# Second attention of a two-block kernel: separate order plans for VectorE and ScalarE, values of two query blocks together, and the gating constant from sums of rows

## The chip, the cores and the metric

The kernel runs on one core of a Trainium2 chip. The metric is the device time of one execution in microseconds (us), the median of several runs. The engines of the core are TensorE (PE: matmuls; PEld: its weight loads), VectorE (DVE), ScalarE (ACT), GpSimd (POOL) and SyncE (SP, which here only issues DMAs). Each engine works through its own list of instructions in order; they meet only through semaphores.

## The reference, cut to what matters

Two transformer blocks run one after the other over 512 positions of width 1024, all in float32. The change touches two places of the second block:

```python
def gmlp_spatial_gating(z_u, z_v, ln_g, ln_b, w_s, b_s):
    v = layernorm(z_v, ln_g, ln_b)               # ... * g + b, per channel c
    w = where(mask, w_s, 0)                      # 8 groups, 128 x 128
    mixed = einsum('gts,bnsgc->bntgc', w, v) + b_s.T[None, None, :, :, None]
    return z_u * mixed

def forgetting_attention(q, k, v, f_logit, b_f): # 16 heads of 64, query blocks of 128
    for i in range(4):
        s = q[block i] . k[: end of block i] / 8 + cum[t] - cum[s]
        s = where(causal, s, -1e30)
        prob = softmax(s)
        out[block i] = prob . v
```

The bias `ln_b` of the layernorm goes through `w_s` as a constant that doesn't depend on the data: for group g, channel c and position t it is ln_b[g, c] * sum over s of w[g, t, s], plus b_s[g, t]. The kernel works this "gating constant" `e_s` out early, stores it in DRAM and loads it back when the gating is due.

## The kernel before, in words

Activations lie transposed, channels on the 128 partitions, 512 positions in the free dimension. Every weight tile (128 x 1024) is loaded by SP into one of a few raw buffers, and split: ScalarE writes a rounded high part (`split_hi`, L1111), VectorE the rest (`prepare`, L1572). A product is three matmuls (high times high, low times high, high times low), each at one pass with 512 columns, so a tile of eight chunks takes 24 matmuls, all issued at L609. There are six split buffers, so a split may run up to six tiles ahead of its use; a raw buffer is loaded again once its tile is split.

**The second attention** is woven into 20 main tiles (480 matmuls at L609). Its unit of work is n = 0 .. 63: four query blocks of two heads for each of eight pairs c = n // 8; i = n % 8 // 2 is the query block, so a unit has 128 (i+1) key columns. For each unit:

1. TensorE, `fox_scores(n)`: two score matmuls (L781, L784) and a small bf16 mask matmul (L989) into bank 4 or 5.
2. VectorE, `fox_scores(n)` (L2020): adds the decay row, writes `at_p`, takes the row minimum.
3. ScalarE, `fox_scores(n)` (L1452): exponential, with the row sum.
4. VectorE: reciprocal (L2023) and scaling of `at_p` (L2025).
5. TensorE, `fox_turn(n)` (L1000): i+1 transposes of full precision into the one bank 6. It waits for step 4 of the unit and for step 6 of unit n-1.
6. ScalarE, `fox_turn(n)` (L1459): copy out to `at_pt`.
7. TensorE, `fox_values(n)` for odd n (L1014): for both heads of the pair, products of full precision with `at_pt`, each on half of the array's columns (128*64).

`mix2_order` (L255) writes one list of events for all engines. Step n of it issues turn n-2, scores n and, where n is odd, values n-4, in this order, and then lets through some main matmuls (`woven`, L213): 5 to 9 for each step. Where a main tile ends, the list has "evac" (ScalarE and VectorE take it out of its bank: for a tile of queries two half-tiles each, L1226 and L1753; for keys two half-tiles each, L1235 and L1761, and two copies on VectorE, L1765) and "end" (one weight tile is split, L1111 and L1572). All three engines walk the same list, so on VectorE the pieces of "evac" and "end" stand as one block between two units, and steps 2 and 4 of a unit stand together: between them VectorE waits for step 3.

Queries and keys of pair c are double-buffered; TensorE may start scores of pair c when all their pieces are done.

**The gating constant** is made by `constant(x)` on TensorE (L842), called within the first feed-forward behind unit m = 7 of 22. For each of the eight groups it is a product `lnb` x `ws_s` (L851, contraction over 128 rows) and a product of a row of ones with the row `bs_row` (L852, contraction over one row), both of full precision. ScalarE copies the two banks to `e_s` (L1321), GpSimd stores it.

## Time and profile before

| | us |
|---|---|
| median of 3 runs | 2108.72 (2106.93 to 2109.04) |
| the profiled execution: its own time | 2107.84 |
| its span in the trace | 2106.0 |
| TensorE busy in the span | 2054.4 |
| VectorE busy | 1104.9 |
| ScalarE busy | 807.7 |
| mean granted clock of TensorE | 0.991 of full speed |

The span is the time from the first to the last record of the trace; the execution's own time has 1.84 us around it. The second attention lies between 1260.7 and about 1450 us of the span, the gating constant between 133.96 and 140.98 us.

In a timeline a row is a run of equal instructions: start, length from the first start to the last end, engine, line, what is written from what, shape, count, and in brackets the idle time before it with the engine and line that ended it. Full-precision products show two records for each matmul. Ends of matmuls are modelled; starts are not.

### The profile page before, as it was taken

What the parts mean: (1) busy time and instruction counts of PE and PEld (TensorE: products, weight loads), DVE (VectorE), ACT (ScalarE), POOL (GpSimd) and SP (SyncE); (2) the same over time, 40 slices, a digit from 0 to 9 for tenths busy, and PEclk for the clock granted to TensorE, in tenths of its full rate; (3) what the DMA queues carried; (4) which work ended last, traced back from release to release, by engine and by line L of the source; (5) the groups of instructions that cost most, each with busy time, mean ns of one, the idle gap of its engine ahead of it and who ended that gap; (6) DMA issues with size and microseconds to landing.
All of it is one profiled execution on the core that took longest, in us unless ns stands there. A gap on an engine that the chain in (4) does not pass through costs nothing.

```text
span 2106.0 us, 25140 instructions
## 1 busy us (share of the span) xinstructions
PE 2054.4 (98%) x10227; PEld 1714.1 (81%) x10227; DVE 1104.9 (52%) x1678; ACT 807.7 (38%) x1256; POOL 116.0 (6%) x139
## 2 busy tenths in 40 slices
PE   6999999999999999999999999999999999999997
PEld 4788888888888888888888887778888888888887
DVE  8734444577854554333335546664524476446546
ACT  4422222345544333222224345555323354234334
POOL 3100000100000010000002000000000100000012
PEclk8999999999999999999999999999999999999999
DMA  7744443433432323233223332222332222232241
GB/s 279 248 146 148 172 149 125 166 122 117 142 110 92 98 61 120 75 103 112 88 70 100 112 114 81 71 71 83 98 99 91 81 95 87 90 119 94 69 148 41
DMA packets 70164, 236.27 MB, mean 112 GB/s; under 512 B 7825, under 2 KB 10129, under 8 KB 69666
## 3 DMA queue, kind: packets, MB, share of 16 engines
q1 hardware_dynamic: 67874, 226.59, 32.3%
q0 software_dynamic: 2032, 7.90, 1.1%
q8 instruction: 81, 1.33, 0.3%
q10 hardware_dynamic: 144, 0.18, 0.0%
q14 instruction: 33, 0.27, 0.0%
HBM read 229.89 MB, written 4.75 MB: 111 GB/s over the span
## 4 chain that ended last, share of the span: by engine, by line
PE 90%; DVE 5%; ACT 2%; DMA 1%; issue 1%; POOL 0%; DVEq 0%; SPq 0%; ACTq 0%
PE bank L609 80%; PE bank L673 4%; PE bank L896 1%; DVE w_lo L1572 1%; PE bank L1014 1%; PE bank L1000 1%; ACT at_p L1452 1%; PE bank L781 1%; PE bank L784 1%; DVE raw_m L1568 1%; DMA w_raw<-in_w_mix_dram 0%; PE bank L926 0%; DVE at_p L2020 0%; DVE ssq L1588 0%; DVE klb L1761 0%
## 5 line engine op out<-in xcount | busy, mean ns | idle before, releaser
L1572 DVE TENSOR_TENSOR w_lo<-w_raw,w_hi 128x1024 fp32r<-128x1024 f32 (+2 forms) x367 | 418.4, 1168 | 215.7 <-ACT w_hi L1111 214.8
L609 PE MATMUL bank<-u_lo,w_hi 128*128 128x512 f32 (+1 forms) x1920 | 496.9, 371 | 11.7 <-DVE u_lo L1852 4.9
L609 PE MATMUL bank<-u_hi,w_hi 128*128 128x512 f32 (+1 forms) x1920 | 499.3, 373 | 8.7 <-ACT ff_s L1191 3.6
L609 PE MATMUL bank<-u_hi,w_lo 128*128 128x512 f32 (+1 forms) x1920 | 496.5, 371 | 0.0
L1111 ACT ACTIVATE w_hi<-w_raw 128x1024 fp32r<-128x1024 f32 (+2 forms) x368 | 347.4, 976 | 260.2 <-PE bank L609 194.8
L609 PEld LDWEIGHTS bank<-u_lo,w_hi 128*128 128x128 f32 x1920 | 357.1, 189 | 75.7 <-DVE u_lo L1852 5.7
L609 PEld LDWEIGHTS bank<-u_hi,w_hi 128*128 128x128 f32 x1920 | 358.5, 190 | 72.2 <-ACT ff_s L1191 4.0
L609 PEld LDWEIGHTS bank<-u_hi,w_lo 128*128 128x128 f32 x1920 | 358.6, 190 | 60.9 <-issue 1.7
L1690 DVE TENSOR_TENSOR ff_a<-ff_s,bank 128x512 f32<-128x512 f32 x44 | 30.3, 688 | 233.1 <-issue 220.2
L1185 ACT ACTIVATE act_hi<-ff_a 128x512 fp32r<-128x512 f32 x66 | 41.7, 632 | 256.8 <-DVE ff_a L1690 216.7
L609 PE MATMUL bank<-act_hi,w_lo 128*128 128x512 f32 (+1 forms) x561 | 131.4, 379 | 0.0
L609 PE MATMUL bank<-act_lo,w_hi 128*128 128x512 f32 (+1 forms) x561 | 130.0, 378 | 0.0
L609 PE MATMUL bank<-act_hi,w_hi 128*128 128x512 f32 (+1 forms) x561 | 129.4, 376 | 0.0
L2150 POOL TENSOR_TENSOR ssq<-ssq,sq 128x512 f32<-128x512 f32 (+1 forms) x41 | 50.6, 1235 | 1371.9 <-ACT sq L1136 1371.2
L609 PEld LDWEIGHTS bank<-act_hi,w_lo 128*128 128x128 f32 x561 | 102.1, 189 | 19.3
L609 PEld LDWEIGHTS bank<-act_lo,w_hi 128*128 128x128 f32 x561 | 102.0, 190 | 19.3
L609 PEld LDWEIGHTS bank<-act_hi,w_hi 128*128 128x128 f32 x561 | 101.4, 188 | 19.5
L1568 DVE CUSTOM_DVE_ANT_0 w_raw<-w_raw,cact_t,vecs_t 128x1024 f32<-128x1024 f32 x66 | 87.2, 1327 | 0.4 <-DMA w_raw<-in_w_ada_dram 0.4
L1136 ACT ACTIVATE sq<-hres 128x512 f32<-128x512 f32 (+1 forms) x60 | 33.0, 552 | 116.3 <-DVE hres L1660 68.9
L1716 DVE TENSOR_TENSOR act_lo<-ff_a,act_hi 128x512 fp32r<-128x512 f32 x66 | 45.8, 693 | 51.1 <-ACT act_hi L1185 51.1
L1705 DVE SCALAR_TENSOR_TENSOR ff_c<-bank,vecs_t,ff_c 128x511 f32<-128x511 f32 (+1 forms) x44 | 33.0, 749 | 60.3 <-ACT ff_c L1199 59.4
L1191 ACT ACTIVATE ff_s<-bank 128x512 f32<-128x512 f32 x44 | 26.2, 595 | 94.2 <-PE bank L609 94.2
(273 smaller groups left out, 2129.4 us busy)
## 6 DMA issues: line engine op xcount, KB each, us to landing
w_raw<-in_w_gu_dram SPq DMA_DIRECT2D x127, 512.0 KB, 4.0
w_raw<-in_w_ada_dram SPq DMA_DIRECT2D x66, 512.0 KB, 4.5
w_raw<-in_w_dn_dram SPq DMA_DIRECT2D x48, 384.0 KB, 3.1
w_raw<-in_w_mix_dram SPq DMA_DIRECT2D x36, 512.0 KB, 3.9
w_raw<-in_w_dn_dram SPq DMA_DIRECT2D x48, 320.0 KB, 3.2
w_raw<-in_w_in_dram SPq DMA_DIRECT2D x24, 512.0 KB, 3.5
w_raw<-in_w_o_dram SPq DMA_DIRECT2D x16, 512.0 KB, 3.5
w_raw<-in_w_in_g_dram SPq DMA_DIRECT2D x16, 512.0 KB, 3.5
```

Of the source, the lines that this page charges most:

```text
L609: m = e.matmul(bank[b][:, c], w, (x.lo if part == 2 else x.hi)[:, k, c], start=start, stop=stop, skip_group_check=True)
L673: m = e.matmul(bank[b][:, :], (x.lo if part == 1 else x.hi)[:, k, P * i:P * (i + 1)], w, start=k == 0 and part == 0, stop=k == 2 * len(til ...
L1111: e.activation(hi_of(name), raw_of(i), ACT.Copy).then_inc(*s_w_hi.inc(name))
L1136: e.activation((sq, sq2)[x][d % 2][:, c], hres[:, d, c], ACT.Square, **kw).then_inc(*s_sq.inc(*keys))
L1185: e.activation(act_hi[:, i, :], ff_a[m % 3][:, :], ACT.Copy).then_inc(*s_a_hi.inc((tag, h, i)))
L1191: e.activation(ff_s[m % 3][:, :], psum(f"{tag}g{m}")[:, :], ACT.Silu).then_inc(*s_silu.inc((tag, m)))
L1568: e.tensor_tensor_reduce(raw_of(i), raw_of(i), cact[:, :], 1.0, vecs[:, c:c + 1], ALU.mult, ALU.add, mod[:, name:name + 1]).then_inc(*s_ad ...
L1572: e.tensor_tensor(lo_of(name), raw_of(i), f32(hi_of(name)), ALU.subtract).then_inc(*s_w_lo.inc(name))
L1690: e.tensor_tensor(ff_a[m % 3][:, :], ff_s[m % 3][:, :], psum(f"{tag}u{m}")[:, :], ALU.mult).then_inc(*s_glu.inc((tag, m)))
L1705: e.scalar_tensor_tensor(dst[:, n:T], src[:, 0:T - n], vec("conv_w_2", 44 * k + col), dst[:, n:T], ALU.mult, ALU.add).then_inc(*s_conv.inc ...
L1716: e.tensor_tensor(act_lo[:, i, :], ff_a[m % 3][:, :], f32(act_hi[:, i, :]), ALU.subtract).then_inc(*s_a_lo.inc((tag, h, i)))
L2150: e.tensor_tensor(ssq[x][:, c], ssq[x][:, c], (sq, sq2)[x][d % 2][:, c], ALU.add).then_inc(*s_ssq_pool.inc(*keys))
```

## The change: what it does

- `mix2_order`: the values of two query blocks stand together, in step n with n % 4 = 2, ahead of the turn: values n-5 and n-3 there, then turn n-2, scores n. The order ends after 67 steps rather than 68.
- `mix2_scalar_order` and `mix2_vector_order` (new) derive an own list for ScalarE and VectorE. What "evac" and "end" asked for is cut into pieces (half a tile of queries or keys, one copy, one split, one result) in a queue. ScalarE does one piece behind each scores, two where more than two are left. VectorE does one piece between step 2 and step 4 of a unit (`divide`, cut off from `fox_scores`), and a second one behind step 4 where more than two are left; it takes a piece only if ScalarE has its part in an earlier step.
- The gating constant: two full-precision matmuls of 512 columns with a stationary tile of ones sum the masked rows of `ws_s`; VectorE (no longer ScalarE) forms sum * lnb + bs in eight instructions behind unit m = 8. `bs_all` is now the row b_s broadcast to 128 partitions (512 KB, as `lnb` was before), `lnb` a [128, 8] tile loaded one word at a time (1024 words).

The signatures and declarations around it (`ps=BOTH`, `lnb_t`, the removed `one_row`) are left out of the diff:

```diff
@@ -257,14 +258,14 @@
     steps = []
-    for n in range(64 + 4):
+    for n in range(64 + 3):
         s = []
+        if n >= 6 and n % 4 == 2:
+            s += [("values", n - 5), ("values", n - 3)]
         if 2 <= n < 66:
...
             s.append(("scores", n))
-        if n >= 5 and n % 2:
-            s.append(("values", n - 4))
         steps += [s] + [[]] * (share[n % 8] - 1)
@@ -286,6 +287,65 @@
     return out
+def mix2_scalar_order(events):
+    out, later, when = [], deque(), {}
+    def piece(n):
+        if later:
+            when[later[0]] = n
+            out.append(later.popleft())
+    for what, i in events:
+        j = MIX2[i] if what in ("evac", "end") else 0
+        if what == "evac":
+            later.extend([("zu", i)] if j < 8 else [("query" if j < 24 else "key", (j, p)) for p in BOTH])
+        elif what == "end":
+            later.append(("split", i))
+        elif what == "turn":
+            out.append(("turn", i))
+        elif what == "scores":
+            out.append(("scores", i))
+            piece(i)
+            if len(later) > 2:
+                piece(i)
+    while later:
+        piece(64)
+    return out, when
+def mix2_vector_order(events, when):
+    out, later = [], deque()
+    def piece(n):
+        if later and later[0][1] < n:
+            out.append(later.popleft()[0])
+    for what, i in events:
+        j = MIX2[i] if what in ("evac", "end") else 0
+        if what == "evac" and 8 <= j < 24:
+            later.extend((("query", (j, p)), when["query", (j, 1)]) for p in BOTH)
+        elif what == "evac" and j >= 24:
+            later.extend((("key", (j, p)), when["key", (j, 1)]) for p in BOTH)
+            later.extend((("copy", (j, p)), when["key", (j, 1)]) for p in BOTH)
+        elif what == "end":
+            later.append((("split", i), when["split", i]))
+        elif what == "values" and i % 8 == 7:
+            later.appendleft((("result", i), 0))
+        elif what == "scores":
+            out.append(("scores", i))
+            piece(i)
+            out.append(("divide", i))
+            if len(later) > 2:
+                piece(i)
+    while later:
+        piece(65)
+    return out
 def gating_order():
@@ -842,16 +903,10 @@
             open_bank(b)
+            q.wait_ge(s_const, "eps")
             q.wait_ge(s_ws_mask, 0)
-            q.wait_ge(s_lnb_in, 0)
-            q.wait_ge(s_bs_in, 0)
-            for i in range(4):
-                g = 4 * x + i
-                o = bank[b][:, P * i:P * (i + 1)]
-                e.matmul(o, lnb[:, P * g:P * (g + 1)], ws_s[:, g, :], start=i == 0, stop=False, skip_group_check=True)
-                m = e.matmul(o, one_row[:, :], bs_row[:, P * g:P * (g + 1)], start=False, stop=True,
-                             skip_group_check=True)
-            m.then_inc(*s_out.inc(("const", x)))
+            e.matmul(bank[b][:, :], ones[:, :].to_broadcast([P, P]), ws_s[:, 4 * x:4 * x + 4, :].rearrange("p g c -> p (g c)"),
+                     start=True, stop=True, skip_group_check=True).then_inc(*s_out.inc(("const", x)))
             frees[b] = [(s_e, x)]
@@ -1216,21 +1269,21 @@
                         pump(name)
-        def queries(ph, c, key, scale):
+        def queries(ph, c, key, scale, ps=BOTH):
             s = c % 2
...
                 q.wait_ge(s_out, ("scores", 2 * c - 3, A0) if ph == "a" else ("fox", 8 * c - 9))
-            for p in range(2):
+            for p in ps:
                 own = slice(64 * p, 64 * p + 64)
                 e.activation(qs_t[s][p][own, :], psum(key)[own, :], ACT.Copy, scale=scale).then_inc(*s_q_hi.inc((ph, c, p)))
-        def keys(ph, c, key):
+        def keys(ph, c, key, ps=BOTH):
             s = c % 2
...
                 q.wait_ge(s_out, ("scores", 2 * c - 3, A0) if ph == "a" else ("fox", 8 * c - 9))
-            for p in range(2):
+            for p in ps:
                 own = slice(64 * p, 64 * p + 64)
@@ -1314,13 +1367,7 @@
                 split_hi()
-
-        def constants():
-            for x in range(2):
-                q.wait_ge(s_out, ("const", x))
-                e.activation(e_s[:, 4 * x:4 * x + 4, :], rows_view[6 + x], ACT.Copy).then_inc(*s_e.inc(x))
-
-        ffn("1", "n1", swiglu, beside=constants)
+        ffn("1", "n1", swiglu)
         q.wait_ge(s_e_out, 0)
@@ -1460,17 +1507,18 @@
         table(LOG_EXP)
-        for what, i in mix2_events:
-            if what == "evac":
+        for what, i in mix2_scalar:
+            if what == "zu":
                 j = MIX2[i]
-                if j < 8:
-                    q.wait_ge(s_out, (f"n{j}", None))
-                    e.activation(zu[j][:, :], psum(f"n{j}")[:, :], ACT.Copy).then_inc(*s_zu.inc(j))
-                elif j < 24:
-                    queries("b", j % 8, f"n{j}", -0.125)
-                else:
-                    keys("b", j % 8, f"n{j}")
-            elif what == "end":
+                q.wait_ge(s_out, (f"n{j}", None))
+                e.activation(zu[j][:, :], psum(f"n{j}")[:, :], ACT.Copy).then_inc(*s_zu.inc(j))
+            elif what == "query":
+                j, p = i
+                queries("b", j % 8, f"n{j}", -0.125, (p,))
+            elif what == "key":
+                j, p = i
+                keys("b", j % 8, f"n{j}", (p,))
+            elif what == "split":
                 pump(f"n{MIX2[i]}")
@@ -1722,8 +1770,8 @@
                     pump(f"{tag}u{max(m, first_pairs[tag] - 1)}")
-                    if beside and m == 5:
-                        beside()
+                    if beside and m in beside:
+                        beside[m]()
                 if h == 0 and half:
@@ -1745,22 +1793,29 @@
                         pump(key + "b")
-        def queries(ph, c, key, scale):
+        def queries(ph, c, key, scale, ps=BOTH):
             s = c % 2
             q.wait_ge(s_q_hi, (ph, c, 1))
-            for p in range(2):
+            for p in ps:
                 own, other = slice(64 * p, 64 * p + 64), slice(64 - 64 * p, 128 - 64 * p)
...
         def keys(ph, c, key):
+            key_lows(ph, c, key)
+            key_copies(ph, c)
+        def key_lows(ph, c, key, ps=BOTH):
             s = c % 2
             q.wait_ge(s_k_hi, (ph, c, 1))
-            for p in range(2):
+            for p in ps:
                 own = slice(64 * p, 64 * p + 64)
                 e.tensor_tensor(kl_t[ph][s][p][own, :], psum(key)[own, :], f32(ks_t[s][p][own, :]),
                                 ALU.subtract).then_inc(*s_kl.inc((ph, c, p)))
-            for p in range(2):
+        def key_copies(ph, c, ps=BOTH):
+            s = c % 2
+            for p in ps:
                 own, other = slice(64 * p, 64 * p + 64), slice(64 - 64 * p, 128 - 64 * p)
@@ -1859,7 +1913,20 @@
             e.memset(ws_s[64:128, :, 0:64], 0.0).then_inc(*s_ws_mask.inc(0))
-        ffn("1", "n1", swiglu, lambda d, h: x_ready("n0", d), half_gate(0), half=(0, 0), beside=constant_mask)
+        def constants():
+            q.wait_ge(s_lnb_in, 0)
+            q.wait_ge(s_bs_in, 0)
+            for x in range(2):
+                q.wait_ge(s_out, ("const", x))
+                for i in range(4):
+                    g = 4 * x + i
+                    m = e.scalar_tensor_tensor(e_s[:, g, :], bank[6 + x][:, P * i:P * (i + 1)], lnb[:, g:g + 1],
+                                               bs_all[:, g, :], ALU.mult, ALU.add)
+                m.then_inc(*s_e.inc(x))
+        ffn("1", "n1", swiglu, lambda d, h: x_ready("n0", d), half_gate(0), half=(0, 0),
+            beside={5: constant_mask, 8: constants})
         q.wait_ge(s_e_out, 0)
@@ -2019,23 +2086,32 @@
                                    mneg[:, col]).then_inc(*s_fmin.inc(n))
+        def fox_divide(n):
+            i, p = n % 8 // 2, n % 2
+            pt, col = at_p[p][:, 0:P * (i + 1)], slice(n % 8, n % 8 + 1)
             q.wait_ge(s_fexp, n)
...
             e.tensor_scalar(pt, pt, rinv[:, col], None, op0=ALU.mult).then_inc(*s_fe.inc(n))
-        for what, i in mix2_events:
-            if what == "evac":
-                j = MIX2[i]
-                if 8 <= j < 24:
-                    queries("b", j % 8, f"n{j}", -0.125)
-                elif j >= 24:
-                    keys("b", j % 8, f"n{j}")
-            elif what == "end":
+        for what, i in mix2_vector:
+            if what == "query":
+                j, p = i
+                queries("b", j % 8, f"n{j}", -0.125, (p,))
+            elif what == "key":
+                j, p = i
+                key_lows("b", j % 8, f"n{j}", (p,))
+            elif what == "copy":
+                j, p = i
+                key_copies("b", j % 8, (p,))
+            elif what == "split":
                 pump(f"n{MIX2[i]}")
             elif what == "scores":
                 fox_scores(i)
-            elif what == "values" and i % 8 == 7:
+            elif what == "divide":
+                fox_divide(i)
+            elif what == "result":
                 q.wait_ge(s_out, ("values", "b", i))
@@ -2309,8 +2385,9 @@
         e.dma_start(ws_s[:, :, :], io["ws"]).then_inc(*s_ws_in.inc(0, by=16))
-        e.dma_start(lnb[:, :], io["ln_b"].to_broadcast([P, D])).then_inc(*s_lnb_in.inc(0, by=16))
-        e.dma_start(bs_row[:, :], io["b_s"]).then_inc(*s_bs_in.inc(0, by=16))
+        e.dma_start(bs_all[:, :, :].rearrange("p g c -> p (g c)"), io["b_s"].to_broadcast([P, D])).then_inc(*s_bs_in.inc(0, by=16))
+        with nc.allow_non_contiguous_dma("one word of the norm's bias for each partition and group"):
+            e.dma_start(lnb[:, :], io["ln_b"].rearrange("o (g c) -> c (o g)", c=P)).then_inc(*s_lnb_in.inc(0, by=16))
         e.dma_start(b_f[:, :], io["b_f"]).then_inc(*s_bf_in.inc(0, by=16))
```

## Rows read from the trace of the kernel before

**Rows 1.** The page, busy us of each engine (share of the span).

```profile
PE 2054.4 (98%) x10227; PEld 1714.1 (81%) x10227; DVE 1104.9 (52%) x1678; ACT 807.7 (38%) x1256; POOL 116.0 (6%) x139
```

**Rows 2.** Windows, whole second attention: from:to, length, busy us per engine, PEclk.

```profile
1260.70:1449.00 188.30, 181.43 (x1126) 140.22 (x1125) 114.28 (x320) 104.40 (x244) 6.56 (x12) 1.00 0.23 71
```

**Rows 3.** Waits, same stretch: who waits for whom, us, times, longest.

```profile
DVE rinv_t L2023 <- ACT at_p L1452: 46.2, 64, 0.9
...
PE bank L1000 <- DVE at_p L2025: 6.1, 6, 1.3
...
PE bank L1000 <- ACT at_pte L1459: 0.6, 1, 0.6
```

**Rows 4.** Timeline of TensorE: start us, us, line, tiles, count, idle before.

```profile
1290.38 1.84 PE L609 MATMUL bank<-u_hi,w_lo 128*128 128x512 f32 x7
1293.56 0.41 PE L1000 MATMUL bank<-ident_t,at_p 128*128 128x128 f32 x2 [1.33 <-DVE at_p L2025]
```

**Rows 5.** Timeline of VectorE ahead of that idle.

```profile
1288.16 1.41 DVE L1761 TENSOR_TENSOR klb<-bank,ks 64x512 fp32r<-64x512 f32 x2 [0.55 <-ACT ks L1235]
1289.60 0.88 DVE L1765 CAST ks<-ks 64x512 fp32r<-64x512 f32 x2
1290.51 1.23 DVE L1572 TENSOR_TENSOR w_lo<-w_raw,w_hi 128x1024 fp32r<-128x1024 f32 x1
1291.76 0.42 DVE L2020 CUSTOM_DVE_ANT_0 at_p<-bank,at_c 128x256 f32<-128x256 f32 x1
```

**Rows 6.** Timeline of TensorE: mask to second main matmul, three steps.

```profile
1276.52 0.23 PE L989 MATMUL bank<-mask_b,ident_b 128*128 128x128 bf16 x1
...
1277.60 2.00 PE L609 MATMUL bank<-u_hi,w_hi 128*128 128x512 f32 x8
...
1297.22 0.23 PE L989 MATMUL bank<-mask_b,ident_b 128*128 128x128 bf16 x1
...
1297.57 2.02 PE L609 MATMUL bank<-u_hi,w_hi 128*128 128x512 f32 x8
...
1359.45 0.23 PE L989 MATMUL bank<-mask_b,ident_b 128*128 128x128 bf16 x1
...
1360.98 1.11 PE L609 MATMUL bank<-u_hi,w_lo 128*128 128x512 f32 x4
```

**Rows 7.** Timeline of TensorE: values straight behind main matmuls.

```profile
1449.19 0.63 PE L609 MATMUL bank<-u_lo,w_hi 128*128 128x512 f32 x2
1449.75 1.09 PE L1014 MATMUL bank<-at_pto,v_b 128*64 128x128 f32 x16
```

**Rows 8.** Timeline of VectorE: one step of 512 columns.

```profile
1276.79 0.69 DVE L2020 CUSTOM_DVE_ANT_0 at_p<-bank,at_c 128x512 f32<-128x512 f32 x1 [0.30 <-PE bank L989]
...
1278.57 0.49 DVE L2025 TENSOR_SCALAR at_p<-at_p,rinv_t 128x512 f32<-128x512 f32 x1
```

**Rows 9.** Timeline of TensorE around the gating constant.

```profile
133.96 0.38 PE L851 MATMUL bank<-ws_s,lnb 128*128 128x128 f32 x2
...
140.98 3.78 PE L609 MATMUL bank<-u_hi,w_hi 128*128 128x512 f32 x8
...
147.39 1.99 PE L609 MATMUL bank<-u_lo,w_hi 128*128 128x512 f32 x8
...
149.21 1.07 PE L609 MATMUL bank<-u_hi,w_hi 128*128 128x512 f32 x4
```

**Rows 10.** Windows, last us of the constant.

```profile
140.00:141.00 1.00, 1.00 (x5) 0.55 (x4) 0.11 (x2) 0.00 (x0) 0.00 (x0) 0.50 0.73 121
```

**Rows 11.** Timeline of TensorE: four full-precision products of 128 columns.

```profile
1457.71 1.05 PE L1046 MATMUL bank<-ws,zv 128*128 128x128 f32 x8
...
1458.52 2.07 PE L609 MATMUL bank<-u_hi,w_hi 128*128 128x512 f32 x8
```

**Rows 12.** Timeline of VectorE in the first feed-forward.

```profile
134.22 0.69 DVE L1690 TENSOR_TENSOR ff_a<-ff_s,bank 128x512 f32<-128x512 f32 x1 [4.98 <-issue]
```

**Rows 13.** The page, DMA queues: packets, MB, share of 16 engines.

```profile
q1 hardware_dynamic: 67874, 226.59, 32.3%
```

13 lines of the change are left out of this document (6 added, 7 removed).

## The prediction

> **What bounds the kernel now.** I read the busy times first. TensorE is busy 2054.4 of 2106.0 us, VectorE and ScalarE about half and a third [rows 1]. So a change pays only where it shortens what TensorE issues, where TensorE stands idle, or where its clock is low; work taken from VectorE or ScalarE is worth what TensorE stops waiting for.
>
> Then the windows. In the second attention TensorE is busy 181.43 of 188.30 us at full clock [rows 2]: 6.87 us idle. The waits name it: transposes (L1000) wait six times for VectorE's scaling of at_p (6.1 us, at most 1.3 each), once for ScalarE's copy (0.6) [rows 3], and once more for 0.2. There are eight such gaps. A gap is longer than its bracket, because ends are modelled. Main matmuls start 0.2275 us apart (eight in 1.82 us, the last two of [rows 9]). In the gap shown [rows 4] the second of seven starts 0.35 us behind its mask (below), so the eighth start would be at about 1292.05; the transpose starts at 1293.56: 1.5 us, not 1.33. With 0.2 us more for each of eight gaps the stalls are 8.3 us.
>
> What makes them is in VectorE's list ahead of the gap [rows 5]: 1.41 us of keys, 0.88 of copies and 1.23 of a split stand in one block, 3.6 us from 1288.16 to 1291.76, and only then comes step 2 of the next unit. Meanwhile VectorE itself waited 46.2 us in the stage, 64 times up to 0.9, for ScalarE's exponential between its steps 2 and 4 [rows 3].
>
> Last, the timeline and the clock around the gating constant. TensorE has left the main matmuls at 133.96 and is back at 140.98 [rows 9]: 7.02 us for 16 small products. In the last of these us the granted clock is 0.50, so 1.2 GHz instead of 2.4 [rows 10], and the two groups of eight behind it take 147.39 - 140.98 = 6.41 us where sixteen at full clock take 3.64 [rows 9]: 2.77 us more. TensorE was not idle before the clock fell; it had issued 6 us of short products, every second over one row of the array.
>
> **The change, part by part.**
>
> *1. Gating constant, TensorE.* Removed: 7.02 us. Added: two full-precision matmuls of 512 columns. Four full-precision products of 128 columns on the whole array, 512 columns together, take 1458.52 - 1457.71 = 0.81 us [rows 11], so two of 512 are 1.62. With about 0.2 us for entering and leaving I take 1.8. The bounds are half of it and double: 0.9, if those rows are held up by their eight weight loads and not by the columns, and 3.5, if the clock is at 1.2 GHz. Saved: 5.2 (3.5 to 6.1).
>
> *2. Gating constant, clock.* With full-height, full-width matmuls in place of the short ones I expect no fall at 140 us: 2.77 us saved. The bounds are 0 (it falls all the same) and 3.3 (0.5 us of the constant also ran slow, already in part 1). I take 2.8. Parts 1 and 2 together: 8.0.
>
> *3. Gating constant, elsewhere.* ScalarE loses two copies, which no one waited for. VectorE gains eight instructions of 128 columns; the nearest row is 0.42 us for 256 columns [rows 5], so at most 3.4 us. They stand behind unit m = 8, where VectorE then waits 5 us for TensorE in each unit [rows 12]; that wait hides them. If the cover were gone they would cost up to 3.4. GpSimd stores the constant a few us later, and it is wanted only at the end of the first feed-forward and again 1300 us later. On SP's queue the broadcast keeps its size, but the 1024 words of lnb are new: every weight load behind them waits. A packet of this queue takes 0.323 * 16 * 2106 / 67874 = 0.16 us on average [rows 13]; 64 on each of 16 engines would be at most 10 us. Five split tiles of 24 * 0.2275 = 5.46 us stand ahead of TensorE, 27 us, so 10 us are hidden. I take 0, and keep the other end for a rival.
>
> The Trainium skill ("DMA: Bandwidth & Descriptors", section "Why a DMA increments its semaphore by 16 and not by 1") lets the slowest dimension of both sides, here 128, set how many engines share a transfer: 16. By that rule the delay is the hidden one; a transfer of so small pieces is not in the trace of before, so no row here shows it yet.
>
> *4. Values in pairs.* A values group between a mask and main matmuls costs TensorE more than its matmuls. From mask to second main matmul it is 0.35 us without values (1297.22 to 1297.57), 1.08 with eight records (1276.52 to 1277.60), 1.53 with sixteen (1359.45 to 1360.98) [rows 6]. So eight cost 0.73 and sixteen 1.18: 0.056 for each record and 0.28 fixed for the group. Half as many groups (16 for 32) save 16 * 0.28 = 4.5 us, if a pair costs one fixed part. Now the group stands behind main matmuls of 512 columns, not behind a small mask, and ahead of a transpose. The entry is the same: behind two main matmuls the values start at 1449.75, where the third would have started at 1449.65 [rows 7]. The exit into a transpose is in no row; it may cost its weight load more, some 0.1 us, 1.6 over sixteen. I take 4.0 (bounds 1.0 and 4.5).
>
> The Trainium skill ("TensorEngine Tiling (Array Packing)", section "Tiling Modes", "Key Properties") says that a change of tiling mode drains the engine. By it a group entered behind 512 columns would drain longer than behind 128 and the pair would save little; the entry of 0.1 us in rows 7 speaks against that, and by the rule's strictest reading the sum would be 3 us smaller.
>
> *5. Own orders for VectorE and ScalarE.* Walking the new list step by step: VectorE never has more than two pieces in a unit, and one of them lies in a gap of up to 0.9 us in which it used to wait. A heavy unit (512 columns) was 1.79 us from step 2 to the start of step 4, plus 0.49 [rows 8], so 2.3; with a split in the gap it is 2.6, with one more half-tile 3.3, against 2.3 + 3.6 before. TensorE gives a unit 2.9 us there (nine main matmuls 2.05, transposes, scores) and two units of slack before the transposes need step 4. Light units (256 columns) last 1.7 us on TensorE and 1.9 to 2.6 on VectorE, but only two in a row, and then comes a pair of values (0.28 + 28 * 0.056 = 1.8 us). So the eight gaps go.
>
> What is late next: (a) scores 32. In the new list the last copy of keys of pair 4 stands behind step 4 of unit 31, and scores 32 wait for it. VectorE is through at 0.27 + 2.27 + 0.44 = 3.0 us behind mask 31, TensorE arrives after nine main matmuls and four transposes, 2.5 us: 0.5 us idle. In all other pairs the last copy stands earlier. (b) ScalarE does turn n-1 behind exp n and a piece, and turn n waits for that copy; where VectorE is two us behind, around units 12 to 16, I expect some 1.5 us in all. Stalls left: 2.0 us (bounds 0.5 and 8). Saved: 8.3 - 2.0 = 6.3.
>
> No cost: the weight splits are done up to two steps later, with five tiles ahead (27 us); banks of main tiles are free at least four steps before they are opened again; behind the last values the order is as before.
>
> **Sum.** 8.0 + 4.0 + 6.3 = 18.3. The profiled execution took 2107.84 (span 2106.0 and 1.84 around it), so 2089.5; its own time is 0.9 below the median shown, so I give the median of the changed kernel as 2090, with 2085 to 2094 for this case alone.
>
> **The rivals.**
>
> *A. The clock still falls at the constant, or falls in the attention.* For it: it fell without idle time before. Against it: at full clock all through the attention, with eight stalls of up to 1.5 us [rows 2]. Price 2.8: 2093.
>
> *B. New waits take the place of the old ones.* Pieces between steps 2 and 4 hold up step 4: a split is 1.23 us [rows 5] in a gap of at most 0.88, so 0.35 later each time; over 20 splits 7.0 us, if every one reaches TensorE. That eats part 5: 2096.5. For it: the transposes already wait for just this result. Against it: two units of slack.
>
> *C. Slower: the 1024 words go through one DMA engine.* Then the loads behind them are held by 1024 * 0.16 = 164 us less 27 of cover: 137 us of standing TensorE, 2227. It decides from where the words hold the queue over 27 + 18 = 45 us, so if fewer than four engines share them or a word costs four times a mean packet. For it: no transfer like it in the trace. Against it: broadcasts over 128 partitions landed as any other load, and the new one is over 128 partitions too.
>
> *D. The values don't pair on TensorE (each pays its fixed part).* 4.0 less: 2094.
>
> **How the numbers follow.** Chances: my forecast 0.62, A 0.09, B 0.15, C 0.03, D 0.09, other small losses 0.02. The range of 8 in 10 leaves out C and part of B: 2084 to 2097. Faster by over 0.2% (4.2 us, about what a measurement of this kernel can tell from no change) needs only a quarter of the sum: 0.95; the same 0.015, slower 0.035.
>
> **What would show it right or wrong.** TensorE between its last main matmul before the constant and the first after it: 1.8 us; clock 1.00 in the 10 us after. Attention: idle of TensorE 1 to 2 us instead of 6.87, one of the gaps ahead of L781 of scores 32, waiting for L1765; 16 blocks of L1014 with 0.26 to 0.36 fixed each; VectorE's wait before L2023 down from 46 to about 20 us. The prediction is wrong if the stage shortens by less than 6 us, if the clock shows 0.50 behind the constant, or if weight splits (L1111) wait for DMA between 110 and 130 us.

## The result and the profile after

The changed kernel takes 2085.06 us (median of four, 2082.51 to 2085.57), the kernel before 2108.41 in the same comparison: ratio 0.9888, 95% interval 0.9871 to 0.9905. That is 23.4 us off, where 18.3 were forecast, and by the interval 20.0 to 27.2; 2085.06 lies in the range of 2084 to 2097, near its lower end. The profiled execution took 2082.51, with a span of 2080.4 us.

The page after, busy us of each engine and the large DMA queue, beside [rows 1] and [rows 13]: TensorE does 14 us less work in a span 25.6 us shorter, and the queue carries 1038 packets more in about the same share of time (32.6 and 32.3%).

```profile
PE 2040.0 (98%) x10199; PEld 1705.3 (82%) x10199; DVE 1106.4 (53%) x1685; ACT 806.8 (39%) x1254; POOL 116.3 (6%) x139
...
q1 hardware_dynamic: 68912, 226.59, 32.6%
```

TensorE around the constant, beside [rows 9], and the window of [rows 10] again. The two matmuls (four records) take 133.56 - 132.25 = 1.31 us; the eight main matmuls behind them take 2.25 for the usual 1.82, 0.43 more. Together 1.74. The clock stays at 1.00.

```profile
132.25 1.88 PE L908 MATMUL bank<-ws_s,ones_t 128*128 128x512 f32 x4
133.56 2.41 PE L670 MATMUL bank<-u_hi,w_hi 128*128 128x512 f32 x8
135.81 1.99 PE L670 MATMUL bank<-u_hi,w_lo 128*128 128x512 f32 x8
```

```profile
140.00:141.00 1.00, 1.00 (x6) 0.84 (x5) 0.00 (x0) 0.24 (x1) 0.00 (x0) 1.00 1.00 406
```

VectorE's eight instructions for `e_s` cost 0.27 us each (the timeline of VectorE, behind unit m = 8):

```profile
150.08 2.16 DVE L1924 SCALAR_TENSOR_TENSOR e_s<-bank,lnb_t,bs_all 128x128 f32<-128x128 f32 x8
```

The window of the second attention without its first and last pieces, beside [rows 2]: TensorE is idle 0.37 us, 6.87 before.

```profile
1248.80:1424.30 175.50, 175.13 (x1116) 137.58 (x1115) 112.62 (x319) 103.01 (x243) 6.58 (x12) 1.00 0.25 76
```

The waits there, beside [rows 3]. L2094 is the line that was L2023, L842 was L781. VectorE's wait for the exponential went from 46.2 us in 64 pieces to 18.7 in 34, since pieces now fill it; in return it waits 35.4 us for the next scores: it is early. TensorE has one wait left.

```profile
DVE at_p L2087 <- PE bank L1044: 35.4, 34, 2.3
DVE rinv_t L2094 <- ACT at_p L1499: 18.7, 34, 0.9
...
PE bank L842 <- DVE ks L1820: 0.3, 1, 0.3
```

That wait on TensorE's timeline, and VectorE's beside it. Scores 32 wait for the second copy of keys, which stands behind `divide` of unit 31 (the TENSOR_SCALAR). Unhindered, they would start 0.35 to 0.36 us behind the first of the four transposes, at 1333.13 (as at 1270.36 and 1270.71 in the fence after this one); they start at 1333.71, 0.58 late.

```profile
1332.77 0.60 PE L1055 MATMUL bank<-ident_t,at_p 128*128 128x128 f32 x4
1333.71 0.30 PE L842 MATMUL bank<-ks,qs 128*128 128x128 f32 x1 [0.35 <-DVE ks L1820]
```

```profile
1332.62 0.49 DVE L2096 TENSOR_SCALAR at_p<-at_p,rinv_t 128x512 f32<-128x512 f32 x1
1333.14 0.42 DVE L1820 CAST ks<-ks 64x512 fp32r<-64x512 f32 x1
```

A pair of values on TensorE's timeline, behind five main matmuls: twelve and sixteen records in one block, entered and left once.

```profile
1270.36 0.60 PE L1055 MATMUL bank<-ident_t,at_p 128*128 128x128 f32 x4
1270.71 0.31 PE L842 MATMUL bank<-ks,qs 128*128 128x128 f32 x1
...
1271.01 1.40 PE L670 MATMUL bank<-u_lo,w_hi 128*128 128x512 f32 x5
1272.34 0.88 PE L1069 MATMUL bank<-at_pte,v_b 128*64 128x128 f32 x12
1273.05 1.04 PE L1069 MATMUL bank<-at_pto,v_b 128*64 128x128 f32 x16
1274.02 0.33 PE L1055 MATMUL bank<-ident_t,at_p 128*128 128x128 f32 x1
```

**Where the time went, stage by stage.** The chain of waits joins unbroken work of TensorE into blocks (start us, us, engine, tile, line, records). Four of them recur in every trace and serve as marks. Of before:

```profile
141.05 271.37 PE bank L609 x1200
...
630.01 140.68 PE bank L609 x655
...
1173.43 87.04 PE bank L673 x384
...
1479.39 196.01 PE bank L609 x900
```

and of after:

```profile
134.12 268.53 PE bank L670 x1200
...
616.62 140.68 PE bank L670 x655
...
1161.57 87.04 PE bank L734 x384
...
1454.70 196.01 PE bank L670 x900
```

From the first product of the constant (133.96, 132.25) to the end of the first block: 278.46 and 270.40 us, 8.06 less. From the end of the 87.04 block to the start of the 196.01 block, which is the second attention: 218.92 and 206.09, 12.83 less. These two hold what the change touches. The other 4.7 us of the two spans lie outside it: 3.6 of them between the first block and the 140.68 one (217.59 and 213.97), 1.7 ahead of the constant (133.96 and 132.25), 0.9 behind the start of the 196.01 block, and 1.5 the other way between the starts of the 140.68 block and the 87.04 one (543.42 and 544.95). The experiments had to tell what of all this is the change's.

### The profile page after: what moved, and what is told of

Same layout as the page of the kernel before. It is cut to its first block, busy times and chain, and to the rows that moved or that the text cites. A ratio compares the mean times of both kernels' runs of the same rounds, so it can differ in the third digit from the quotient of the medians.

```text
span 2080.4 us, 25071 instructions
## 1 busy us (share of the span) xinstructions
PE 2040.0 (98%) x10199; PEld 1705.3 (82%) x10199; DVE 1106.4 (53%) x1685; ACT 806.8 (39%) x1254; POOL 116.3 (6%) x139
## 3 DMA queue, kind: packets, MB, share of 16 engines
q1 hardware_dynamic: 68912, 226.59, 32.6%
q8 instruction: 81, 1.33, 0.3%
## 4 chain that ended last, share of the span: by engine, by line
PE 94%; DVE 3%; ACT 1%; DMA 1%; issue 0%; POOL 0%; DVEq 0%; SPq 0%; ACTq 0%
PE bank L670 82%; PE bank L734 5%; PE bank L1069 1%; PE bank L1055 1%; PE bank L951 1%; PE bank L842 1%; PE bank L845 1%; DVE raw_m L1616 1%; DMA w_raw<-in_w_gu_dram 0%; PE bank L981 0%; DVE w_raw L1616 0%; DVE ssq L1636 0%; PE bank L1101 0%; PE bank L755 0%; PE bank L764 0%
## 5 line engine op out<-in xcount | busy, mean ns | idle before, releaser
L734 PE MATMUL bank<-w_hi,u_hi 128*128 128x512 f32 x160 | 62.3, 389 | 0.0
```

The source lines that it names most:

```text
L734: m = e.matmul(bank[b][:, :], (x.lo if part == 1 else x.hi)[:, k, P * i:P * (i + 1)], w, start=k == 0 and part == 0, stop=k == 2 * len(til ...
```

## The experiments

Medians are of runs beside the kernel before on one chip, and a ratio is to its median there: 2108.41 beside the changed kernel, 2107.60 beside constant alone to tall constant, 2108.15 beside gap unused to attention alone, 2106.84 beside the last three. "Constant" and "attention" are the two stretches just defined, and "between" the one from the end of the first block to the start of the 140.68 one, from each kernel's own trace.

| kernel | median us | ratio to before [95%] | constant | between | attention |
|---|---|---|---|---|---|
| before | 2108.41 | | 278.46 | 217.59 | 218.92 |
| changed | 2085.06 | 0.9888 [0.9871, 0.9905] | 270.40 | 213.97 | 206.09 |
| constant alone | 2096.39 | 0.9952 [0.9940, 0.9965] | 270.41 | 213.38 | 218.96 |
| pairs alone | 2106.64 | 0.9996 [0.9986, 1.0006] | 279.85 | 214.72 | 218.74 |
| plans alone | 2099.67 | 0.9964 [0.9951, 0.9977] | 279.90 | 218.10 | 210.46 |
| tall constant | 2100.15 | 0.9967 [0.9955, 0.9978] | 272.23 | 216.13 | 218.92 |
| gap unused | 2092.39 | 0.9926 [0.9913, 0.9940] | 270.40 | 213.32 | 213.89 |
| copy early | 2085.09 | 0.9894 [0.9878, 0.9910] | 270.41 | 214.32 | 205.52 |
| changed again | 2084.65 | 0.9890 [0.9876, 0.9904] | 270.41 | 214.15 | 206.09 |
| attention alone | 2095.54 | 0.9941 [0.9928, 0.9953] | 279.89 | 215.24 | 206.11 |
| before again | 2111.62 (one) | | 279.91 | 218.33 | 218.95 |
| more words | 2107.64 | 1.0001 [0.9989, 1.0013] | 279.86 | 213.98 | 218.93 |
| constants moved | 2084.91 | 0.9901 [0.9885, 0.9917] | 270.41 | 215.23 | 206.10 |
| few words | 2083.75 | 0.9890 [0.9875, 0.9906] | 270.41 | 214.18 | 206.08 |

**Constant alone.** The new constant and its loads in the kernel before:

```diff
-                e.matmul(o, lnb[:, P * g:P * (g + 1)], ws_s[:, g, :], start=i == 0, stop=False, skip_group_check=True)
-                m = e.matmul(o, one_row[:, :], bs_row[:, P * g:P * (g + 1)], start=False, stop=True,
...
+            e.matmul(bank[b][:, :], ones[:, :].to_broadcast([P, P]), ws_s[:, 4 * x:4 * x + 4, :].rearrange("p g c -> p (g c)"),
...
```

> The kernel before with the new gating constant alone; the attention keeps its old order. Theory 1 (the parts add): TensorE is away from its main matmuls for about 1.7 us instead of 7.02, the clock shows 1.00 behind it, the eight gaps of the attention (6.9 us of idle) stay; 8.0 us faster, so 2100 to 2101. Rival (the clock's fall is only moved, because it comes where it comes in any order): 5.3 us faster, and a stretch at 0.50 shows within the 10 us behind the constant. Rival of the 1024 words: weight splits wait for DMA between 105 and 130 us.

Measured: 270.41 in the constant's stretch, the attention unchanged. TensorE's timeline has the same rows as the changed kernel, 1.31 us and then the 2.41 us group:

```profile
134.15 1.88 PE L846 MATMUL bank<-ws_s,ones_t 128*128 128x512 f32 x4
135.46 2.41 PE L608 MATMUL bank<-u_hi,w_hi 128*128 128x512 f32 x8
```

Theory 1 held. The ratio says 10.1 us (7.4 to 12.6 by its interval, so 8.06 is not excluded); before again (below) shows why it may be more than 8.06.

**Tall constant.** The old constant, with its second product over 128 rows (`lnb` and `ws_s` again) in place of one row, so that `b_s` is left out of it:

```diff
-                m = e.matmul(o, one_row[:, :], bs_row[:, P * g:P * (g + 1)], start=False, stop=True,
+                m = e.matmul(o, lnb[:, P * g:P * (g + 1)], ws_s[:, g, :], start=False, stop=True,
```

> The kernel before, where the second product of each group of the constant (a row of ones with the row of b_s, contraction over one row) is the first product once more, over 128 rows; b_s is left out of the result. Sixteen small full-precision products as before, all on the whole array. Theory A (the one-row products make it slow and let the clock fall): 16 products at about 0.2 us, 3.3 us instead of 7.02, no clock of 0.50 behind it: 3.7 + 2.8 = 6.5 us faster. Theory B (short products in themselves do both): still about 7 us, clock 0.50 behind it, no difference in time. Between them: 3.3 us, but the clock falls all the same: 3.7 faster.

The same count of products of the same width, but each pair of records starts 0.22 us behind the last (0.31 once and then 0.41 to 0.42 with the one-row products in between, up to the clock's fall, as in before again below), the whole is 136.46 - 132.97 = 3.49 us, and the clock is 1.00 throughout. The timeline of TensorE, first two products, last, and what follows:

```profile
132.97 0.38 PE L851 MATMUL bank<-ws_s,lnb 128*128 128x128 f32 x2
133.19 0.39 PE L852 MATMUL bank<-ws_s,lnb 128*128 128x128 f32 x2
...
136.31 0.39 PE L852 MATMUL bank<-ws_s,lnb 128*128 128x128 f32 x2
136.46 2.07 PE L609 MATMUL bank<-u_hi,w_hi 128*128 128x512 f32 x8
```

So without the one-row products both losses are gone, the slow issue and the clock fall; the stretch is 7.7 us shorter than in the other traces of the old constant (279.9, below), where Theory A said 6.5. The two wide matmuls save another 1.8 us (272.23 - 270.41). Two things stay open. The steps of 0.41 us go from a one-row product to a full one as well as the other way, so the rows don't tell whether the one-row product itself is slow or the change between the two shapes. And the products are through in 3.49 us here, while in the six traces of the old constant the clock fell 3.1 to 5.9 us behind the first of them: that the shorter stretch, and not its full height, kept the clock up is not excluded by this one trace.

**Pairs alone.** Only `mix2_order` as in the change, the engines' orders as before:

```diff
+        if n >= 6 and n % 4 == 2:
+            s += [("values", n - 5), ("values", n - 3)]
-        if n >= 5 and n % 2:
-            s.append(("values", n - 4))
```

> The kernel before with the values of two query blocks together, all engines still walking one list; old constant. Theory 1: 16 fixed parts of about 0.28 us fall away, 4.0 to 4.5 us faster, the gaps ahead of the transposes stay at 6 to 8 us. Rival 1 (each group pays its fixed part also in a pair): no difference within 0.5 us. Rival 2 (pairs give VectorE the time it lacked in light units, so part of the stall gain is theirs): 6 us or more faster, idle of TensorE in the stage under 5 us.

The attention is 0.18 us shorter, where 4 were expected: the theory that the pairs pay by themselves fell. The number is that of rival 1 (no difference within 0.5 us), but not for its reason, as the next run shows. TensorE now has eleven gaps, 8.99 us idle in the window, 8.8 of them named in the waits, the longest 2.27 with the granted clock at 0.55 for the 3.8 us behind it. Waits, the longest gap, and the window behind it:

```profile
PE bank L1000 <- DVE at_p L2025: 6.5, 6, 2.3
PE bank L1000 <- ACT at_pte L1459: 1.2, 2, 0.6
PE bank L1014 <- ACT at_pto L1459: 0.8, 2, 0.6
PE bank L1000 <- ACT at_pto L1459: 0.3, 1, 0.3
```

```profile
1361.21 0.66 PE L1000 MATMUL bank<-ident_t,at_p 128*128 128x128 f32 x2 [2.27 <-DVE at_p L2025]
```

```profile
1361.20:1365.00 3.80, 3.79 (x12) 2.97 (x13) 1.88 (x8) 1.58 (x5) 0.00 (x0) 0.55 0.08 32
```

An account from these rows: 9.0 us of idle time in the brackets, 0.2 more for each of eleven gaps, and 3.8 * 0.45 = 1.7 of slow clock are 12.9. The stretches of two later runs that have no wait of TensorE left give the same by subtraction. Copy early has the pairs and takes 205.52, so pairs alone loses 218.74 - 205.52 = 13.2 us; plans alone has no pairs and takes 210.46, so before loses 218.92 - 210.46 = 8.5. The pairs saved 4.9 us of work, and 4.8 us of new stalls took it back. That these stalls were hidden before, behind the separate values groups, is my reading and not shown by itself.

**Plans alone.** The two engines' own orders, values as before:

```diff
+    mix2_scalar, scalar_when = mix2_scalar_order(mix2_events)
+    mix2_vector = mix2_vector_order(mix2_events, scalar_when)
```

> The kernel before with the own plans of VectorE and ScalarE alone; values as before, one group in every second step; old constant. Theory 1: the gaps go but for about 0.5 us at scores 32: 7.7 us faster, idle of TensorE in the stage under 1 us. Rival (the plans need the paired values, whose 1.8 us ahead of a light unit let VectorE catch up): 3 to 6 us faster, with gaps ahead of transposes that wait for VectorE's scaling or ScalarE's copy.

The attention is 8.46 us shorter, where Theory 1 said 7.7, and TensorE has no gap in it at all, not at scores 32 either (window; why scores 32 come in time here was not looked into):

```profile
1262.80:1442.60 179.80, 179.78 (x1125) 140.89 (x1124) 111.40 (x318) 105.22 (x244) 6.58 (x12) 1.00 0.23 71
```

Against it the changed kernel is 210.46 - 206.09 = 4.37 shorter with 0.58 of stall: the pairs save 4.95 us there, 0.31 for each of the sixteen groups that are gone.

**Gap unused.** The changed kernel, VectorE's pieces all behind `divide`:

```diff
             out.append(("scores", i))
-            piece(i)
             out.append(("divide", i))
+            piece(i)
             if len(later) > 2:
                 piece(i)
```

> The changed kernel, with one thing moved in VectorE's order: its pieces of keys, queries, natural products and values all stand behind `divide` of the unit, none in the gap between a unit's scores and `divide`. ScalarE keeps its own order. Theory (heads first is what matters: TensorE's next scores wait for `softmax_head`, and a piece in the gap is only a convenience): the stage keeps nearly all of its gain, 0.5 to 2 us more than the changed kernel's 206.09 us between the landmarks, nearly all of it where a last copy of keys or queries now stands behind a `divide` (scores 32 waited 0.58 us there already). Rival (the gap between scores and `divide`, some 19 us of VectorE's waiting over the stage, is what carries the pieces; without it VectorE runs behind at every unit): 4 to 8 us more, with VectorE as what TensorE waits for at many units, and the wait for `rinv_t` back towards the 46 us of the kernel before.

The theory fell on size: the attention takes 213.89, 7.80 more, and VectorE's wait for the exponential is back at 46.4 us, as the rival said. But the rival's "at many units" isn't there either. There are five gaps. The waits of TensorE, its longest gap and the window behind it:

```profile
PE bank L842 <- DVE ks L1820: 3.1, 2, 2.0
PE bank L1069 <- ACT at_pto L1506: 1.9, 2, 1.1
PE bank L1055 <- ACT at_pto L1506: 0.2, 1, 0.2
```

```profile
1338.87 0.30 PE L842 MATMUL bank<-ks,qs 128*128 128x128 f32 x1 [1.97 <-DVE ks L1820]
```

```profile
1338.90:1342.50 3.60, 3.60 (x11) 2.92 (x12) 2.39 (x6) 0.97 (x3) 0.00 (x0) 0.53 0.07 22
```

No transpose waits for VectorE's scaling any more, which was the old fault. What is late are the last copies of keys (two gaps, scores 32 now 1.97) and, probably by way of late scores, ScalarE's copies of the turns; 5.3 us in the brackets, 1.0 for five ends and 3.6 * 0.47 = 1.7 of slow clock make 8.0, for 8.37 against copy early, which has no stall (213.89 - 205.52). Before had 8.5 us of stalls. So pieces spread behind `divide` remove the old waits and put as much in their place, and the 5.03 us that this kernel gains on before are the pairs' alone; the pieces in the gap remove the new waits too.

**Copy early.** A half-tile piece of VectorE waits for its own half only:

```diff
-            later.extend((("key", (j, p)), when["key", (j, 1)]) for p in BOTH)
+            later.extend((("key", (j, p)), when["key", (j, p)]) for p in BOTH)
-            q.wait_ge(s_k_hi, (ph, c, 1))
+            q.wait_ge(s_k_hi, (ph, c, ps[-1]))
```

(and the same for queries).

> The changed kernel, but a piece of VectorE's that copies one half of a tile of queries or keys waits for that half's product alone, not for both halves, and is placed in the order by that. The one gap that is left in the stage of the changed kernel (scores 32 wait for the last copy of keys, 0.58 us behind the row ahead) should then close. Theory: the late copy is that gap's whole cause, so the stage is 0.3 to 0.6 us shorter than 206.09 us and no other gap opens. Rival: the copy only changes places with `divide` of the unit before, whose scores come late instead, and the stage stays within 0.2 us. By the times of the whole kernel neither can be told from no change (0.03%); the rows decide.

The attention takes 205.52, 0.57 less: the theory held. No wait of TensorE is left in it. Its window:

```profile
1251.40:1425.50 174.10, 174.08 (x1115) 137.10 (x1114) 112.55 (x319) 102.80 (x241) 6.58 (x12) 1.00 0.25 76
```

It is ahead of the changed kernel only in this stage of the trace; by the medians (2085.09 and 2084.65) the two can't be told apart.

**Changed again, attention alone.** The first is the changed kernel unaltered; the second has the old constant.

> The changed kernel once more, unaltered, timed beside the kernel before on one chip with five rounds, and profiled a second time. Theory (the change gives 8.0 us at the constant and 12.8 us in the second attention, and the 4.7 us above that in the first profile are clock falls and a start that differ from one execution to the next in stages that the change doesn't touch): the two changed stages come out within 0.3 us of 270.40 and 206.09, the others move by up to 4 us in either direction, and the median stands 18 to 24 us under the kernel before. Rival (the change also shortens a stage between, by what it leaves in a queue): the stretch of 213.97 us between the two attentions' landmarks is there again within 0.3 us.

> The kernel before with both attention parts of the change (own plans, values in pairs) and the old gating constant. Theory (the parts add up: the constant ends 1100 us before the stage begins): the stage takes 206.1 us between the landmarks, 12.8 less than before, the constant 278.4 us as before with its clock fall to 0.50 behind it, and the whole is 12 to 14 us faster than before. Rival (what the pairs seemed to add, 4.4 us over the plans alone, was partly the pieces' new places in the one kernel): 8.5 to 11 us.

Both changed stages are there again to 0.02 us, and 23.5 us under before by the medians, as expected. Attention alone gives 206.11, so the 4.4 us over plans alone don't hang on the one kernel; its constant's stretch missed the expected 278.4 by 1.5 (below), and the ratios add up: 4.8 for the constant alone and 5.9 for the attention alone are 10.7 in a thousand (22.6 us); the whole is 11.0. The stretch between came out at 214.15 beside 213.97: that is what the rival said (within 0.3); my theory had let it move by up to 4 us, and one more trace doesn't tell the two apart.

**Before again, more words, constants moved, few words.** These ask whether the new constant also shortens the stretch between, and by which of its traits. More words adds the 1024-word load to before; constants moved pads the changed kernel so that its tiles lie where they did; few words loads `lnb` with 128 packets of 32 bytes, thus a wrong bias, in the changed kernel.

```diff
 more words, in before:
...
+            e.dma_start(lnb_t[:, :], io["ln_b"].rearrange("o (g c) -> c (o g)", c=P))
...
 constants moved, in the changed kernel:
+    pad = const("pad_t", [1, P], F32)
 few words, in the changed kernel:
...
-            e.dma_start(lnb[:, :], io["ln_b"].rearrange("o (g c) -> c (o g)", c=P))
...
+        e.dma_start(lnb[:, :], io["ln_b"][:, 0:ND].to_broadcast([P, ND]))
...
```

> The kernel before, unaltered, profiled again. The stretch from the last main matmul of the first pair of the feed-forward (at 412.42 us before) to the first matmuls of the 140.68 us block took 217.59, 214.72, 218.10, 215.24 and 216.13 us in the five traces with the old constant or the tall one, and 213.3 to 214.3 in the five with the new one. Theory (the new constant also shortens this stretch, by way of its transfers): it takes over 214.6 us here too, with over 4.3 us from the last issue of `w_mix` ahead of the stop to the next. Rival (chance): under 214.4.

> The kernel before with one transfer more, behind the load of `bs_row`: the 1024 words of `ln_b`, eight to a partition, into a tile that nobody reads. TensorE, ScalarE and VectorE do what they did before. Theory (the 1024 single words leave the DMA engines in another turn, and that shortens a transfer of `w_mix` from 4.4 to 5.3 us down to 3.6 in the next attention's boundary): the stretch behind the 412.42 us mark takes 213 to 214.4 us, and the kernel is 2 to 3 us faster than before. Rival (the words cost and give nothing): 214.7 to 218.1 us and a ratio of 1.000 +- 0.001.

> The changed kernel with a pad of 512 bytes among its constants, so that every tile of the arena lies where it did before the change. Theory (where tiles lie is indifferent): the stretch takes 213.3 to 214.4 us as in the changed kernel, the constant's stage 270.4 and the second attention's 206.1. Rival (addresses decide the transfers' duration): 214.7 to 218.1 us in that stretch.

> The changed kernel, but `lnb_t` takes the first eight words of `ln_b` in every partition (128 packets of 32 bytes instead of 1024 of one word), so the norm's bias is a wrong one. Theory (the single words shorten the later stretch): it takes 214.7 to 218.1 us and the kernel is 2 to 3 us slower than the changed one. Rival (they have no part in it): 213.3 to 214.4 us, and the kernel's ratio to before stays at 0.989.

Before again settles another point. Its constant's stretch is 279.91, and so is that of every further trace with the old constant (279.85 to 279.91); the profile that I predicted from, 278.46, was the lucky one. In before again the clock falls earlier in the constant, within the pair of records that starts at 138.19 us, 3.6 us behind the first product (5.7 in the first profile); the steps go from 0.41 to 0.73 us. TensorE is back at the main matmuls after 143.13 - 134.56 = 8.57 us, not 7.02:

```profile
134.56 0.38 PE L851 MATMUL bank<-ws_s,lnb 128*128 128x128 f32 x2
...
137.78 0.49 PE L851 MATMUL bank<-ws_s,lnb 128*128 128x128 f32 x2
138.19 0.66 PE L852 MATMUL bank<-bs_row,one_row 1*128 1x128 f32 x2
138.78 0.80 PE L851 MATMUL bank<-ws_s,lnb 128*128 128x128 f32 x2
...
143.13 3.78 PE L609 MATMUL bank<-u_hi,w_hi 128*128 128x512 f32 x8
```

So the constant gives 9.5 us (279.9 - 270.4) in five of six traces; that most executions are of this kind is an inference from these.

The stretch between: before again was 218.33, as its theory said (over 214.6). More words was 213.98 in one trace, as its theory said, yet no faster than before (1.0001), as its rival said; few words stayed at 214.18 and a ratio of 0.9890. The single words have no part in it. Constants moved gave 215.23, outside the 213.3 to 214.4 of its theory and in its rival's range, but its ratio is no worse. With it the two groups overlap: 213.98 to 218.33 (mean 216.3, seven traces with the old or the tall constant) and 213.32 to 215.23 (mean 214.1, seven with the new). The differences have two sources that can be seen. One is a clock fall behind the 1.4 us in which TensorE waits for the norm there, in five of the seven old traces and in one of the seven new. Constants moved is that one. The same ten us behind the first block, of it and of the changed kernel:

```profile
402.03:412.03 10.00, 8.14 (x54) 7.77 (x53) 5.17 (x18) 2.17 (x6) 2.52 (x5) 0.83 0.26 96
```

```profile
402.65:412.65 10.00, 8.11 (x64) 7.56 (x64) 6.17 (x20) 3.02 (x7) 2.82 (x5) 1.00 0.28 98
```

The other source is 54 to 58 us behind the first block, where scores of the first attention wait for ScalarE's `v_a`, 0.5 to 2.7 us; behind three of these waits (before, plans alone, before again; 1.90 to 2.69 us) the clock falls a second time. Of before and of the changed kernel:

```profile
469.48 0.39 PE L781 MATMUL bank<-qs,ks 128*128 128x256 f32 x1 [1.90 <-ACT v_a L1249]
```

```profile
457.45 0.39 PE L842 MATMUL bank<-qs,ks 128*128 128x256 f32 x1 [1.16 <-ACT v_a L1302]
```

By falls, the fourteen values are 213.3 to 214.7 with none, 215.2 to 216.1 with one, 217.6 to 218.3 with two. The 3.62 us of the first two profiles are 0.97 more idle time, most of it this wait, and 2.65 more busy time of TensorE with the two falls. Whether the constant has any effect on how often the clock falls 270 us later, or on how long the wait for `v_a` is (1.2 to 2.7 us in the old traces, 0.5 to 1.5 in the new), is open; 14 traces don't settle it.

## Why the prediction was right, and where it was off

*1, constant on TensorE: right.* 1.8 us forecast, 1.74 measured, 1.31 of it at the constant and 0.43 in the eight main matmuls behind; the clock is at 1.00.

*2, the clock: right against the one trace, small for the median.* There was no fall, as forecast, and terms 1 and 2 together gave 8.06 us against the profile from which they were read (8.0 forecast). That profile had the fall late. In the five other traces with the old constant it came earlier in the constant and cost 1.4 us more. The prediction took the clock's loss from a single execution, though it treated the fall as something that moves (rival A); the median of before probably held the larger loss already (five of six traces have it).

*3, nothing elsewhere: right.* The 1024 words cost nothing that can be told from noise (more words 1.0001, few words), and no wait of TensorE stands behind VectorE's eight instructions. (The 5 us in which VectorE waits in [rows 12] were put down to TensorE; the row names no engine for them.) Rival C is out: with 1038 packets more the queue is busy 0.326 * 2080.4 = 678 us on each engine, 680 before, and no weight split waits for a transfer between 100 and 135 us.

*4, values in pairs: right only beside part 5.* Forecast 4.0, measured 4.95, 0.31 for each of the sixteen groups. In the pair shown, five main matmuls and 28 records would be through at 1271.01 + 5 * 0.2275 + 28 * 0.056 = 1273.72, and the transposes start at 1274.02, 0.30 later. Of these 0.09 are the first step behind the mask (the second main matmul starts at 1271.33), which is as long without values (1297.26 to 1297.57 in before). So entry and exit together cost 0.21, no more than between a mask and main matmuls (0.28); the exit into a transpose costs nothing extra, and the 0.5 us withheld for it was gain too. The working had the fixed part about right, but it priced the pairs as if they stood alone; alone they give 0.18. Rival D (they don't pair) is out. So is the strictest reading of the rule in the Trainium skill ("TensorEngine Tiling (Array Packing)", section "Tiling Modes", "Key Properties") that a change of mode drains the engine. What entry and exit cost is within that 0.21 us, and the entry behind matmuls of 512 columns takes 0.10 of it (the last slot ends at 1272.24, the values start at 1272.34).

*5, own orders: the step that was mis-sized.* All of the stalls went but 0.58, and with the plans alone all 8.46; 2.0 were forecast to stay. The 8.46 bear out 0.2 us for each gap beyond its bracket: 6.87 + 8 * 0.2 is 8.47, where the prediction wrote 8.3. (a) Scores 32 waiting for the last copy: 0.5 forecast, 0.58 measured, at the unit and on the tile named. (b) 1.5 us from ScalarE's turns behind its pieces around units 12 to 16: none. ScalarE's copies of the turns (L1506) wait 18.2 and 16.1 us for TensorE in the stage, 31 times; ScalarE was early, and I had put its lateness down without a row. Rival B (new waits) did not come: VectorE waits 35.4 us for scores, so it is early. Gap unused shows how near it was: one line moved in the order, and 7.8 us are back.

**The sum.** Forecast 8.0 + 4.0 + 6.3 = 18.3. Measured in the two stages 8.06 + 4.95 + 7.88 = 20.9 against the first profile (8.46 - 0.58 = 7.88), and 9.5 + 12.8 = 22.3 against the other traces of before. The medians differ by 23.4 (20.0 to 27.2 by the interval), so both sums fit and the 18.3 forecast don't. The last us is within what the stretch between does from one execution to the next, or is the open point above. The three misses, 1.4 us of clock, 0.95 of the pairs and 1.4 of the stalls, all lie on one side and don't cancel. That the measured time still lies in the range, 1.1 us from its end, is in part luck: the range was set wide for stalls that would stay, and the time left it almost at the other side.

## What to carry to other kernels

A saving can be worth nothing alone and much beside another: here the fixed costs taken from the bound engine paid 0.2 us alone, and 4.4 once the engine that feeds it no longer worked in blocks. So price an edit of the order against the stalls that it uncovers, and test it alone and together. In a list for a feeding engine, cut the blocks into small pieces and fill the waits that this engine has anyway with them (behind its own steps they only moved the stalls here), and let each piece wait for no more than it reads. And take a clock loss from more than one execution: marks that recur in every trace (here blocks of unbroken work on TensorE) tell which stage a difference lies in and whether it is the change's.

## What the runs showed of the hardware

- Full-precision products of 128 columns, alternately over one row of the array and over 128 rows, start 0.41 us apart; all over 128 rows they start 0.22 us apart (tall constant).
- The granted clock fell to 0.50 with no idle row of TensorE before it in all six traces in which every second product of the constant stands on one row, 3.1 to 5.9 us behind the first (pairs alone starts it at 132.79 and shows 0.84 in the window 135.50 to 136.00). It did not fall with 128 rows, in one trace that has such products for 3.49 us only (tall constant).
- The length of an idle time doesn't by itself tell whether the clock falls. Up to 1.33 us in the second attention left it at 1.00 [rows 2, 4], and so did 2.18 us in pairs alone (ahead of 468.45); behind 1.97 and 2.27 us it was 0.53 and 0.55, and behind 1.4 us at the norm it fell in six of fourteen traces. At the later norm, where TensorE waits 1.32 us and 7 to 9 us later again about 1 us, it fell in twelve of fourteen; before and constant alone are the two without, and their stretch from the 140.68 block to the 87.04 one is 543.42 where the others have 544.7 to 546.5.
- Stages without such a fall repeat to some hundredths of a us (206.08 to 206.11 in five traces, 218.92 to 218.96 in five), while whole executions of one kernel spread over 1.5 to 9 us. The gain of 0.57 us shows in the stage and not in the time of the kernel.
